# First expert pair's tokens picked already transposed, and expert 5's down weights loaded at the end of the attention

## The reference, cut to what matters

```python
x = x + concat([o_gla, o_fnet, o_mla]) @ w_out        # (512, 1024)
t = rms_norm(x, norm2_g)
grp_w, grp_idx = top_k(softmax(t @ w_rg + b_rg), 1)   # 4 groups
e_w, e_idx = top_k(softmax((t @ w_re + b_re) in that group), 2); e_w /= sum(e_w)
for e in range(32):                                   # w_gate, w_up: 1024 x 256; w_down: 256 x 1024
    y += combine[:, e] * ((silu(t @ w_gate[e]) * (t @ w_up[e])) @ w_down[e])
return rms_norm(x + y, final_norm_g)
```

## Time and profile before

| | us |
|---|---|
| median of three executions | 527.29 |
| fastest, slowest | 526.87, 527.69 |
| span of the profiled execution, first to last instruction | 526.4 |
| the profiled execution's own time | not given; the median is 0.9 over the span |
| PE busy | 491.7 (93%) |
| PE weight loads | 271.0 (51%) |
| DVE, ACT, POOL busy | 212.8, 136.9, 75.1 |
| moved by DMA | 139.95 MB, mean 266 GB/s |
| mean granted clock of TensorE | 0.987 |

### The profile page before, as it was taken

One profiled execution on the slowest core, in us unless ns is written; L12 is line 12 of the kernel. 1 busy time (PEld: TensorE's weight loads), 2 busy tenths in 40 slices (PEclk: granted clock), 3 DMA queues, 4 the chain that ended last, 5 costly groups with the idle time before them and its releaser, 6 DMA issues.

```text
span 526.4 us, 7686 instructions
## 1 busy us (share of the span) xinstructions
PE 491.7 (93%) x2924; PEld 271.0 (51%) x2924; DVE 212.8 (40%) x565; ACT 136.9 (26%) x357; POOL 75.1 (14%) x101
## 2 busy tenths in 40 slices
PE   4999999999999999999999899999999978878894
PEld 4446544557765555455447555555555444444431
DVE  3317320666676671116763422223323312233167
ACT  3404211354476661203131111111111101112023
POOL 1000000361100000001113122222222222111000
PEclk9999999999999999999998999999999989999898
DMA  8996000010199004931089999999999999999984
GB/s 291 361 278 254 2 1 0 16 36 2 33 398 404 5 1 177 416 127 41 2 317 361 395 418 415 415 417 414 418 412 417 413 417 416 418 415 415 411 327 160
DMA packets 40134, 139.95 MB, mean 266 GB/s; under 512 B 9848, under 2 KB 12984, under 8 KB 31904
## 3 DMA queue, kind: packets, MB, share of 16 engines
q1 hardware_dynamic: 34752, 131.38, 63.5%
q0 software_dynamic: 4816, 7.85, 4.0%
q10 hardware_dynamic: 528, 0.22, 0.2%
HBM read 130.47 MB, written 16.39 MB: 279 GB/s over the span
## 4 chain that ended last, share of the span: by engine, by line
PE 65%; DMA 16%; SPq 9%; DVE 6%; issue 2%; ACT 1%; DVEq 0%; ACTq 0%; POOLq 0%
PE bank L747 12%; PE bank L1065 12%; DMA EW<-in_moe_w_up 9%; PE bank L933 9%; PE bank L1078 5%; SPq L615 5%; PE bank L906 5%; PE bank L976 3%; SPq L620 3%; PE bank L965 3%; DMA EW<-y_scratch 2%; PE bank L1038 2%; DMA EW<-in_w_in 2%; PE bank L755 1%; PE bank L853 1%
## 5 line engine op out<-in xcount | busy, mean ns | idle before, releaser
L1065 PE MATMUL bank<-EW,WO 128*64 128x256 f32 x640 | 78.5, 401 | 9.8 <-DMA EW<-in_moe_w_up 8.1
L1065 PEld LDWEIGHTS bank<-EW,WO 128*64 128x64 f32 x640 | 47.8, 144 | 35.6 <-DMA EW<-in_moe_w_up 9.8
L747 PE MATMUL bank<-EW,XT 128*128 128x512 f32 (+1 forms) x192 | 64.1, 495 | 0.0
L933 PE MATMUL bank<-WO,XT 128*128 128x512 f32 x128 | 56.6, 595 | 0.0
L1411 ACT ACTIVATE G<-bank 128x128 f32<-128x128 f32 x32 | 8.9, 277 | 178.9 <-PE bank L1065 178.9
L1778 DVE TENSOR_TENSOR G<-G,bank 128x128 f32<-128x128 f32 x32 | 9.2, 287 | 113.1 <-ACT G L1411 113.1
L2002 POOL DMA_INDIRECT y_scratch<-G,sidx x30 | 30.2, 1008 | 159.1 <-DVE G L1791 145.8
L747 PEld LDWEIGHTS bank<-EW,XT 128*128 128x128 f32 x192 | 32.9, 190 | 31.0 <-issue 31.0
L1791 DVE COPY G<-bank 128x512 f32<-128x512 f32 x32 | 22.1, 691 | 45.8 <-PE bank L1078 45.8
L1078 PE MATMUL bank<-EW,G 128*64 128x512 f32 x160 | 38.3, 599 | 0.0
L933 PEld LDWEIGHTS bank<-WO,XT 128*128 128x128 f32 x128 | 23.7, 190 | 27.3 <-issue 27.3
(11 more groups left out here) (295 smaller groups left out, 651.8 us busy)
## 6 DMA issues: line engine op xcount, KB each, us to landing
EW<-in_moe_w_gate SPq DMA_DIRECT2D x20, 1024.0 KB, 21.5
EW<-in_moe_w_up SPq DMA_DIRECT2D x20, 1024.0 KB, 21.4
EW<-in_moe_w_down SPq DMA_DIRECT2D x20, 1024.0 KB, 23.3
y_scratch<-MIX SPq DMA_DIRECT2D x8, 512.0 KB, 9.1
WO<-in_w_out SPq DMA_DIRECT2D x2, 2048.0 KB, 12.3
MIX<-in_moe_w_gate SPq DMA_DIRECT2D x4, 1024.0 KB, 20.6
MIX<-in_moe_w_up SPq DMA_DIRECT2D x4, 1024.0 KB, 22.6
WO<-in_moe_w_gate SPq DMA_DIRECT2D x4, 1024.0 KB, 19.7
```

Of the source, the lines that this page charges most:

```text
L747: mm = pe.matmul(ps[:, 0:width], xnT[:, c, t * P:(t + 1) * P], w_in_sb[:, c, col:col + width], start=(c == 0), stop=(c == C - 1))
L933: mm = pe.matmul(ps[:, :], xnT[:, c, t * P:(t + 1) * P], w_out_sb[:, c, n * 512:(n + 1) * 512], start=(c == 0), stop=(c == C - 1))
L1065: mm = pe.matmul(bank[BLOCK * m:BLOCK * (m + 1), 0:2 * P].rearrange("p (w n) -> p w n", w=2), xeT[:, c, par * BLOCK:(par + 1) * BLOCK], wv ...
```

## The change

1. Pair 0's tokens are formed transposed: for each tile, eight products take a strided set of 128 features of x (`X[:, t, c:D:C]`) as weights and `sel0` as the moving operand. The two copies to SBUF and the eight transposes are gone, and the picks' last products count `xe_full` by half. The semaphores `pick_done` and `picked` are gone; SP (line 652) and POOL's first gather wait for `xe_full` instead.
2. The router's scratch moves out of `G[:, 0:2048]` to places further up and into `ropet`; the output of ACT's squares, which nobody reads, goes to bank 0 in place of `sqh`.
3. Place 5's down weights are loaded right after places 0 and 1, ahead of the stores of x, and without the wait for `weights_ready`.
4. The token numbers of pair 2 are worked out after expert 0's gate and up products; DVE's handling of the last tile's weights moves ahead of its wait for them.

```diff
@@ SyncE
             for s in (0, 1):
                 load_gate_up(s, s)
                 load_down(s, s)
+            load_down(RING + 1, RING + 1)
             for t in range(T):
...
             load_gate_up(RING + 2, RING + 2)
-            sp.wait_ge(pick_done, 1)
+            sp.wait_ge(xe_full, 2)
             sp.wait_ge(x2_stored, 16 * T)
             load_down(RING + 2, RING + 2)
-            sp.wait_ge(weights_ready, 1)
-            load_down(RING + 1, RING + 1)
             sp.wait_ge(gu_full, 1)
@@ TensorE, "pick"
                     pe.wait_ge(sel_ready, 2 * t + 2)
+                    if t == 0:
+                        pe.wait_ge(squares_ready, SQ2 + 2 * T)
...
-                    for n in range(2):
-                        mm = pe.matmul(banks[n][:, :], sel0[:, t].rearrange("p e s -> p (e s)"),
-                                       X[:, t, n * 512:(n + 1) * 512], start=(t == 0), stop=(t == T - 1))
-                    if t == T - 1:
-                        mm.then_inc(pick_done, 1)
+                    for c in range(C):
+                        mm = pe.matmul(banks[c // 4][:, c % 4 * P:(c % 4 + 1) * P], X[:, t, c:D:C],
+                                       sel0[:, t].rearrange("p e s -> p (e s)"), start=(t == 0 and c % 4 == 0),
+                                       stop=(t == T - 1), skip_group_check=True)
+                        if t == T - 1 and c % 4 == 3:
+                            mm.then_inc(xe_full, 1)
@@ TensorE, after the router
-            for pair in (1, 2):
+            def token_numbers(pair):
                 ps = open_bank(("ids", pair))
...
-                if pair == 1:
-                    pe.wait_ge(picked, 2)
-                    for half in range(2):
-                        tokens(0, half).then_inc(xe_full, 1)
+            pe.wait_ge(sel4_ready, T)
+            token_numbers(1)
...
                 gate_up(place, par).then_inc(gu_full, 1)
                 if e == 0:
+                    token_numbers(2)
                     counts()
@@ ScalarE
-                    act.activation(sqh, X[:, t, n * 512:(n + 1) * 512], ACT.Square,
+                    act.activation(banks[0][:, :], X[:, t, n * 512:(n + 1) * 512], ACT.Square,
...
-            act.wait_ge(pick_done, 1)
-            act.wait_ge(x2_stored, 16 * T)
-            act.activation(xg[0][:, 512:D], banks[1][:, :], ACT.Copy).then_inc(picked, 1)
@@ VectorE
-            dve.wait_ge(pick_done, 1)
-            dve.wait_ge(x2_stored, 16 * T)
-            dve.tensor_copy(xg[0][:, 0:512], banks[0][:, :]).then_inc(picked, 1)
+            copy_tokens(0)
             for pair in (1, 2):
...
                 if pair == 1:
-                    copy_tokens(0)
-            link(weights(T - 1))
-            dve.tensor_tensor(held_w, ...).then_inc(weights_ready, 1)
+                    link(weights(T - 1))
+                    dve.tensor_tensor(held_w, ...).then_inc(weights_ready, 1)
@@ GpSimd
             def gather(pair):
-                pool.wait_ge(*((pick_done, 1) if pair == 1 else (xe_full, 2 * pair - 2)))
+                pool.wait_ge(xe_full, max(2 * pair - 2, 2))
```

More of the change, by code:

```diff
@@ L378, in encoder_kernel @@
                                                       X[:, 0:2, :].rearrange("p t n -> p (t n)")]
-        lg = view(G, 0, (T, NG + NE))
-        rt = view(G, 160, (T, 14, NE))
+        sc_at = view(G, 2432, (T, 32))
+        l32_at = ropet[:, :, :, :].rearrange("p a t w -> p (a t w)").rearrange("p (t e) -> p t e", t=T)
+        rows_at = view(G, 3072, (T, 2, NE))
+        lg = view(G, 3328, (T, NG + NE))
         mska = view(G, 2048, (T, NE))
@@ L1387, in _ @@
                     act.wait_ge(logit_ready, 2 * t + 1)
-                    act.activation(rt[:, t, 1, 0:NG], lg[:, t, 0:NG], ACT.Exp, bias=rt[:, t, 0, 3:4],
-                                   accum_out=rt[:, t, 0, 0:1]).then_inc(rexp_ready, 1)
+                    act.activation(sc_at[:, t, 14:14 + NG], lg[:, t, 0:NG], ACT.Exp, bias=sc_at[:, t, 3:4],
+                                   accum_out=sc_at[:, t, 0:1]).then_inc(rexp_ready, 1)
                     act.wait_ge(logit_ready, 2 * t + 2)
-                    act.activation(rt[:, t, 0, 4:5], rt[:, t, 0, 5:6], ACT.Exp).then_inc(rexp_ready, 1)
+                    act.activation(sc_at[:, t, 4:5], sc_at[:, t, 5:6], ACT.Exp).then_inc(rexp_ready, 1)
             act.preload_act_table_set("silu_and_others")
-            act.wait_ge(pick_done, 1)
-            act.wait_ge(x2_stored, 16 * T)
-            act.activation(xg[0][:, 512:D], banks[1][:, :], ACT.Copy).then_inc(picked, 1)
             def copy_half(half):
@@ L1664, in _, with first_max @@
                     free_bank(dve.tensor_copy(xnT[:, 4 + tq, :], ps[:, :]), ("O", tq))
-            def first_max(vals, k, t, r, onehot, m):
+            def first_max(vals, a, k, t, onehot, m):
                 link(dve.tensor_reduce(m, vals, AX, ALU.max))
-                a = rt[:, t, r, 0:k]
-                b = rt[:, t, 0, 12:13]
+                b = sc_at[:, t, 12:13]
                 link(dve.scalar_tensor_tensor(a, vals, m, rank[:, 0:k], ALU.is_equal, ALU.mult))
@@ L1676, in weights @@
             def weights(t):
-                sc = rt[:, t, 0]
+                sc = sc_at[:, t]
                 dve.wait_ge(rexp_ready, 2 * t + 2)
@@ L1707, in _ @@
                     drained(dve, step)
-                    sc = rt[:, t, 0]
-                    ohg, l32 = rt[:, t, 2, 0:NG], rt[:, t, 4]
+                    sc = sc_at[:, t]
+                    ohg, l32, scratch = sc[:, 18:18 + NG], l32_at[:, t], rows_at[:, t, 0]
                     dve.tensor_reduce(sc[:, 3:4], lg[:, t, 0:NG], AX, ALU.max, negate=True).then_inc(logit_ready, 1)
-                    link(first_max(lg[:, t, 0:NG], NG, t, 3, ohg, sc[:, 2:3]))
+                    link(first_max(lg[:, t, 0:NG], sc[:, 22:22 + NG], NG, t, ohg, sc[:, 2:3]))
                     link(dve.tensor_scalar(ohg, ohg, -NBIG, NBIG, ALU.mult, ALU.add))
@@ L1716, in _ @@
                                            ohg.unsqueeze(2).to_broadcast([P, NG, EPG]), ALU.add))
-                    link(first_max(l32, NE, t, 8, oh[:, t, 0], sc[:, 6:7]))
+                    link(first_max(l32, scratch, NE, t, oh[:, t, 0], sc[:, 6:7]))
                     link(dve.scalar_tensor_tensor(l32, oh[:, t, 0], 4 * NBIG, l32, ALU.mult, ALU.add))
-                    link(first_max(l32, NE, t, 9, oh[:, t, 1], sc[:, 7:8]))
+                    link(first_max(l32, scratch, NE, t, oh[:, t, 1], sc[:, 7:8]))
                     dve.tensor_tensor(mska[:, t], oh[:, t, 0], oh[:, t, 1], ALU.add).then_inc(picks_ready, 1)
@@ L1731, in _ @@
                                       ALU.is_equal).then_inc(sel4_ready, 1)
-                    row, rows2 = rt[:, t, 10], rt[:, t, 11:13]
+                    row, rows2 = l32_at[:, t], rows_at[:, t]
                     free_bank(dve.tensor_tensor(row, ps[:, 0:NE], small[:, 0:NE], ALU.add), step)
@@ L1735, in _ @@
                     link(dve.tensor_tensor(rows2, oh[:, t], row.unsqueeze(1).to_broadcast([P, 2, NE]), ALU.mult))
-                    link(dve.tensor_reduce(rt[:, t, 0, 10:12], rows2, AX, ALU.add))
-                    dve.scalar_tensor_tensor(dest[:, t, :], rt[:, t, 0, 10:12], -1.0, rt[:, t, 0, 10:12],
+                    link(dve.tensor_reduce(sc_at[:, t, 10:12], rows2, AX, ALU.add))
+                    dve.scalar_tensor_tensor(dest[:, t, :], sc_at[:, t, 10:12], -1.0, sc_at[:, t, 10:12],
                                              ALU.mult, ALU.max).then_inc(dest_ready, 1)
@@ L1756, in _ @@
                 if pair == 1:
-                    copy_tokens(0)
-            link(weights(T - 1))
-            held_w = nm[:, 0:4 * T].rearrange("p (t e r) -> p t e r", e=2, r=2)
-            dve.tensor_tensor(held_w, oh[:, :, :, NE - 2:NE].rearrange("p t r e -> p t e r"),
-                              wts[:, :, :].unsqueeze(2).to_broadcast([P, T, 2, 2]), ALU.mult).then_inc(weights_ready, 1)
+                    link(weights(T - 1))
+                    dve.tensor_tensor(held_w, oh[:, :, :, NE - 2:NE].rearrange("p t r e -> p t e r"),
+                                      wts[:, :, :].unsqueeze(2).to_broadcast([P, T, 2, 2]), ALU.mult).then_inc(weights_ready, 1)
             def most():
```

5 lines of the change are left out of this document (1 added, 4 removed).

## The result

| | before | changed | ratio |
|---|---|---|---|
| median of four executions (us) | 527.49 | 533.21 | 1.011 (95%: 1.0085 to 1.0135) |
| fastest, slowest (us) | 526.87, 529.9 | 532.8, 536.44 | |
| span of the profiled execution (us) | 526.4 | 531.2 (its own time 533.01) | |

The change made the kernel slower by 1.1%, where 0.5% faster was forecast; 533.21 us is 6.7 us above the range's upper end of 526.5. It went the way of rival D. In nearly all executions that have both figures the time is about 1.8 us over the span, so the profile of the kernel before is, by estimate, of an execution of 528.2 us, above its median: hence the spans differ by 4.8 us and the medians by 5.7.

What follows compares the result with a forecast made beforehand. The prediction took the continuous stream of weight loads after 264 us as the bound. Its sum, 2.5 (moved load) + 0.2 (small hole) - 0.2 (stream dry) = 2.5 us less, gave 524.8 us from 527.29, range 523.9 to 526.5.

Steps and rivals of the forecast that it cites:

- rival D: Picks between first pick and expert 0: 128-column passes cost more than 0.12 us, kernel slower, up to 533 us; chance 0.05.
- the moved load: Expert 5's 1 MiB of down weights moves into idle time at about 229 to 232 us, saving 2.5 us of stream.
- The picks: Router, four tiles: sixteen passes each at 0.12 us, 0.2 us more per tile than before; only tile 3's on the path.
- Hidden or on the path: Tile 0's pick hidden before the logits, at most 0.1 us; tiles 1 and 2 add 0.4 us, just hidden before the position product.
- Copies and transposes removed: Between last pick and expert 0: gate and up products start at about 278.95 us, 1.7 us earlier.
- Clock: Expert 0's gate and up products: full clock expected, 3.67 us instead of 5.36, another 1.7 us.
- The hole: Stream after place 6's down weights, 284.8 us: idle about 2 us unless PE releases expert 7's load earlier; 1.7 to 3.4 expected.
- the stream is dry for 0 to 0.5 us: Before expert 9's data at about 298.6 us: queued loads last until 298.2 us; 0.2 us taken as loss.
- its 3 us: In rival D's total: 3 us subtracted from 527.3 plus a delay of up to 9 us, giving 533 us.
- What the profile would show: Signs: if right, last pick about 2.1 us, expert 0 from about 279 us, expert 7's load at 282.7 us, list read done at 291.
- wrong branch: Signs of failure: stream share well under 0.9 between 284 and 300 us, picks of 4 us, or PE last releasing y's read.
- A: Stream at 284.8 us and 291 to 299 us runs dry, 1 to 2 us go back: 525.8 to 527.0 us; chance 0.17.

Runs made afterwards that it cites:

- kernel 2: The changed kernel with pick weights of 128 features lying side by side instead of strided (pair 0's results not the reference's): 528.55 us, ratio 1.0013.
- kernel 4: The kernel before, with the 32 transposes of x for the logits made float32 products with the identity: 538.68 us, one execution, only durations used.
- kernel 5: The changed kernel with pick weights at step 2 (tile 0), 4 (tile 1), 8 (tile 3), and x at step 8 as moving operand (tile 2): 530.75 us, one execution.
- Kernel 1: The changed kernel with the old picks, copies, transposes and token-number places; early load and moved scratch stay: 528.44 us, ratio 1.0006.
- kernel 9: The same kernel as kernel 8, run again beside kernel 10: 526.58 us, ratio 0.9970.
- kernel 10: Kernel 9 with expert 5's down weights loaded late, as before the change: 527.36 us, ratio 0.9979.
- kernel 8: Kernel 2 plus three unread products of 512 columns, two ahead of the wait for the lists and one behind expert 1: 526.53 us, ratio 0.9977.

## Why the prediction was wrong

Two terms failed: the cost of a pass of the picks, which made the kernel slower, and the worth of the moved load, the 2.5 us of the sum. With the first put right (kernel 2) the time was 528.55 us, still not the 524.8 us of the forecast.

**The picks: the step that failed.** The prediction bounded a pass from above by "eight transposes that load their operand with the same stride", 0.145 us each, and took 0.12. A transpose is one pass and a float32 product two, and the prediction knew it (it counts sixteen passes for eight products), but took a row of the one as a bound for the other. Measured: 0.24 to 0.25 us, twice the forecast and outside the bounds; kernels 2, 4 and 5 show that it is the step. The sum had the picks at 0.2 us on the path; they put 7.4 us there. No row of before had a product with a strided operand, and without one the upper bound should have been the nearest row of a dearer kind, the 0.43 us of a pass of 512 columns, not a row of a cheaper kind.

**Hidden or on the path.** That tile 0's pick is hidden, and those of tiles 1 and 2 "just hidden", was right for 0.12 us with slack of a few tenths of a microsecond. At 0.24 us they put 1.8 and 3.6 us on the path. Kernel 2, at 0.12 us, has the position product at the place where it was before: the slack was real.

**Copies and transposes removed: right.** From the last pick's end to expert 0 the forecast had 1.3 us in place of 3.26, and 1.3 was measured; the forecast's 1.7 us is this less 0.2 for the longer pick. In kernel 2 expert 0 starts at 278.27 us, forecast 278.95.

**Clock.** "I expect the full clock" failed in the changed kernel (5.17 us; clock 0.70 from 284 to 288 us) and held in kernel 2 (3.67 us). In the kernel before it fell at about 281.0 us, 3.5 us after the last pick's end, in which PE had done transposes and products of 2 columns, had waited and had just begun expert 0. In the changed one it fell at about 285.6 us, 1.0 us after the last pick's end, and that pick had passes of 0.25 us. But kernel 5 had such a pick there too, and ran expert 0 in 3.67 us. What made the difference is open.

**The moved load: size wrong.** "A microsecond of DMA time saved anywhere after 264 us is worth a microsecond, if the queue never runs dry" was the right condition, and it was not met. The hole was named, and the forecast counted on PE being 1.7 to 3.4 us early to close it. Kernel 1 shows the price when PE is not early: 2.2 of the 2.5 us by the ledger, and no gain in the times. Even with PE early the load was worth 0.6 us by the means and 0.8 by the medians (kernels 9 and 10), and the step "the stream is dry for 0 to 0.5 us" at expert 9's load was mis-sized: the list read and a fall of the clock at expert 2 were not in the sum (kernel 2: stream all but dry for some 2.5 us).

**Rival D** had the right mechanism and place: a delay of up to 64 x (p - 0.12) us, at p = 0.24 some 7.7 us, and expert 0 began 7.0 us later than forecast. With its 3 us taken off it gives 532.0; measured 533.2. Its bound, slower from p = 0.18 us on, agrees with this, but no run had a p near it. (For p = 0.27 its own formula gives 64 x 0.15 = 9.6 us, not 9.) The chance of 0.05 rested on the transposes. Its reason did not act: with numbers side by side a pass of 128 columns took 0.12 us against 0.43 for 512, 0.28 of it, as the earlier trace rows had shown. The rule that it was weighed by (the Trainium skill, TensorE: Matmul & The Clock Gate, Back-to-back issue gap, 81 against 131 ns) does not describe these products; what made p high is the step.

**"What the profile would show"** held in its wrong branch on two counts: picks of 4 us (D) and stages with a share well under 0.9 between 284 and 300 us (A).

Among the kernels that compute the reference in full none is measurably faster than the one before. The faster ones (kernels 8 to 10) give pair 0's experts x with its features in another order. To have their time with the reference's output, x would have to lie in SBUF with each chunk's 128 features side by side; that was not tried.

## What to carry to other kernels

Before an operand gets a step, look for a row of the same kind of instruction with the same step: a transpose is no bound for a float32 product, and weights with a step of four numbers or eight, or a moving operand with a step of eight, doubled the product here. When a load is moved out of a full stream, write down which release lets the next one follow; if that release does not come earlier too, the saved bytes turn into a hole. Ledgers of bytes over one fixed stretch (40 us here) told here within about a microsecond how far apart the spans of two profiled executions were, before any chain was read; they do not replace repeated times, since the executions of one kernel spread over 2 us and more.

## What was not expected of the hardware

- A float32 product's pass of 128 columns with a step of 2, 4 and 8 numbers between weights: 0.118, 0.238 and 0.25 us. The weight load: 196, 328 and 334 ns.
- The same with the step of 8 on the moving operand, and weights side by side: 0.233 us a pass, at 207 ns a load.
- A transpose's load without a step: 141 ns; at step 2: 208 ns; at step 8: 193 ns.
- A wait of 2.54 us, two products of 32 columns, transposes and a short wait, 1.9 us together, were followed by a granted clock of 0.50, which stood for most of expert 2's product, 6.59 us for 3.67 (kernel 2); two unread products in that wait, and a third behind expert 1, kept it at 1.00 (kernel 8), and the kernel became 2 us faster by doing more.
